# Two buffers for the recurrence's output gate, and stage waits for the PSUM banks that come next

## The reference

```
h = rmsnorm(x) ; x = x + 1/2 * rmsnorm(swiglu(h))            # FFN 1, 2816 hidden
h = rmsnorm(x) ; z = h @ W_in                                # one wide projection
  A: attention, 3 groups (window, dilation) x 8 heads of 64, merged by their softmax sums
  B: 8 heads, each 128 wide, both directions, in chunks of 64 tokens:
       S_t = diag(f_t) S_{t-1} + k_t v_t^T ;  o_t = S_t^T q_t
       o = rmsnorm(o_fwd + o_bwd) * silu(g_h)                # g_h: the output gate
  y = (sigmoid(gate_a) * (A @ P_A) + sigmoid(gate_h) * (B @ P_B)) @ W_out
x = x + rmsnorm(y)
h = rmsnorm(x) ; x = x + 1/2 * rmsnorm(swiglu(h))            # FFN 2
```

## Time and profile before

| | |
|---|---|
| median of 3 runs | 1547.39 us (1547.31 to 1548.15) |
| the profiled execution, its own time | 1546.26 us |
| its span in the profile | 1544.4 us |
| mean granted TensorE clock | 0.994 |
| TensorE matmul busy | 1497.4 us, 97% |
| TensorE weight load busy | 1227.5 us, 79% |
| VectorE busy | 719.4 us, 47% |
| ScalarE busy | 577.2 us, 37% |
| GpSimd busy | 23.5 us, 2% |
| chain that ended last, by engine | PE 94%, ACT 2%, DVE 2%, issue 1% |

### The profile page before, as it was taken

How to read it: one execution, slowest core, us unless ns; L and a number is a source line. 1 busy time by engine, 2 the same in 40 slices (tenths; PEclk the granted TensorE clock), 3 DMA queues, 4 the chain that set the end, 5 groups by cost and what they waited for, 6 DMA issues and landing times.

```text
span 1544.4 us, 20203 instructions
## 1 busy us (share of the span) xinstructions
PE 1497.4 (97%) x7610; PEld 1227.5 (79%) x7610; DVE 719.4 (47%) x1087; ACT 577.2 (37%) x840; POOL 23.5 (2%) x29
## 2 busy tenths in 40 slices
PE   7999999999999999999999999999999999999996
PEld 6888888887987777777887777778876888888885
DVE  6444444224644444443246665654446444443223
ACT  5223323223533444433244554553344332323221
POOL 0000000000100000000000000000000000000001
PEclk9999999999999999999999999999999999999998
DMA  5332222222422222212222221222231222222222
GB/s 182 99 98 95 95 95 95 96 95 82 145 88 90 86 69 86 69 59 92 95 82 69 68 76 60 68 69 96 83 106 57 95 95 95 95 95 95 96 96 82
DMA packets 39186, 138.65 MB, mean 90 GB/s; under 512 B 4535, under 2 KB 4535, under 8 KB 39095
## 3 DMA queue, kind: packets, MB, share of 16 engines
q1 hardware_dynamic: 37440, 132.14, 25.9%
q0 software_dynamic: 1552, 5.76, 1.3%
q10 hardware_dynamic: 144, 0.04, 0.0%
HBM read 135.75 MB, written 2.17 MB: 89 GB/s over the span
## 4 chain that ended last, share of the span: by engine, by line
PE 94%; ACT 2%; DVE 2%; issue 1%; DMA 0%; DVEq 0%; ACTq 0%
PE ps L258 27%; PE ps L259 26%; PE ps L260 26%; PE ps L605 2%; PE ps L848 2%; PE ps L861 2%; PE ps L607 1%; PE ps L606 1%; PE ps L831 1%; PE ps L766 1%; PE ps L768 1%; PE ps L767 1%; PE ps L1147 1%; ACT whi L248 1%; PE ps L1164 1%
## 5 line engine op out<-in xcount | busy, mean ns | idle before, releaser
L258 PE MATMUL ps<-hh,whi 128*128 128x512 f32 x1280 | 510.2, 399 | 26.7 <-DVE hl L520 12.7
L259 PE MATMUL ps<-hl,whi 128*128 128x512 f32 x1280 | 501.1, 391 | 0.0
L260 PE MATMUL ps<-hh,wlo 128*128 128x512 f32 x1280 | 500.8, 391 | 0.0
L248 ACT ACTIVATE whi<-raw 128x1024 fp32r<-128x1024 f32 x242 | 256.1, 1059 | 613.2 <-PE ps L260 552.3
L253 DVE TENSOR_TENSOR wlo<-raw,whi 128x1024 fp32r<-128x1024 f32 x242 | 296.3, 1225 | 396.2 <-ACT whi L248 396.2
L258 PEld LDWEIGHTS ps<-hh,whi 128*128 128x128 f32 x1280 | 241.6, 189 | 88.0 <-issue 28.2
L260 PEld LDWEIGHTS ps<-hh,wlo 128*128 128x128 f32 x1280 | 241.6, 189 | 51.6
L259 PEld LDWEIGHTS ps<-hl,whi 128*128 128x128 f32 x1280 | 241.8, 189 | 48.0 <-issue 0.2
L258 PE MATMUL ps<-ah,whi 128*128 128x512 f32 x352 | 137.1, 389 | 0.8 <-DVE tmp L365 0.8
L259 PE MATMUL ps<-al,whi 128*128 128x512 f32 x352 | 137.0, 389 | 0.0
L260 PE MATMUL ps<-ah,wlo 128*128 128x512 f32 x352 | 136.9, 389 | 0.0
(11 more groups left out here) (216 smaller groups left out, 1528.2 us busy)
## 6 DMA issues: line engine op xcount, KB each, us to landing
raw<-in_wstream SPq DMA_DIRECT2D x244, 512.0 KB, 3.3
bias<-vec_dram POOLq DMA_DIRECT2D x8, 576.0 KB, 6.6
xt<-in_x_t SPq DMA_DIRECT2D x8, 256.0 KB, 5.6
out_t<-xt SPq DMA_DIRECT2D x8, 256.0 KB, 2.0
cst<-in_consts POOLq DMA_DIRECT2D x1, 640.0 KB, 4.9
hot_sb<-in_onehot POOLq DMA_DIRECT2D x1, 297.0 KB, 4.1
vec_dram<-vec_sb POOLq DMA_DIRECT2D x1, 72.0 KB, 2.9
par<-in_params ACTq DMA_DIRECT2D x1, 40.5 KB, 4.1
```

Source lines behind the costliest of these rows:

```text
L248: nc.scalar.activation(whi[:, s, :], raw[:, s, :], ACT.Copy).then_inc(head_done, 1)
L258: nc.tensor.matmul(out, w, m, start=start, stop=False)
L259: nc.tensor.matmul(out, w, ml, start=False, stop=False)
L260: return nc.tensor.matmul(out, wl, m, start=False, stop=stop)
```

## The change

The output gate is made at the end of its own turn, behind the last `head` of that turn, into one of two buffers by the turn's parity (`gate`, and `tmp[:, 1, :]`, which exists already). The loops of ScalarE and VectorE over the turns 2 to 7 become three passes over two turns each; TensorE's loop stays. The v stage's copies out of PSUM are placed ahead of the conversion of the next weight block. Four waits of TensorE between stages become smaller, later or go.

```
+        gates = [gate[:], tmp[:, 1, :]]
...
             for b in range(4):          # v_act; v_dve alike with block_tail
-                if b > 1:
-                    block_head(1, b)
                 if b == 3:
                     leave(1, 0)
                     leave(1, 1)
+                if b > 1:
+                    block_head(1, b)
...
             turn(0, True, False, False)          # hgrn_pe
+            pe.wait_ge(sem("ih_out1"), 5)
             turn(1, True, True, False)
...
-            def turn(h, proj, scan, finish):          # hgrn_act
+            def turn(h, parity, proj, scan, finish):
...
                 if scan:
-                    if finish:
-                        act.wait_ge(sem("b_done"), h)
-                    nc.scalar.activation(gate[:], ps[:, 1, :], ACT.Silu).then_inc(sem("gate_done"), 1)
                     for d in range(2):
...
                 if proj:
                     head(act, first + 2 * h + 1, 1)
-                if not own:
+                if own:
+                    act.wait_ge(block_done, 2 * (first + 2 * h) + 4)
+                    nc.scalar.activation(gates[1 - parity], ps[:, 1, :], ACT.Silu).then_inc(sem("gate_done"), 1)
+                else:
                     nc.scalar.activation(first_gates[3], ps[:, 1, :], ACT.Sigmoid).then_inc(sem("sig_g"), 1)
...
-            with act.Fori(2, GH_HEADS) as h:
-                turn(h, True, True, True)
-            turn(GH_HEADS, True, True, True)
+            with act.Fori(1, GH_HEADS // 2) as two:          # hgrn_dve alike
+                turn(2 * two, 0, True, True, True)
+                turn(2 * two + 1, 1, True, True, True)
+            turn(GH_HEADS, 0, True, True, True)
...
-                nc.vector.scalar_tensor_tensor(out=b_out, in0=ps[:, 5, :], scalar=par[:, 48:49], in1=gate[:],
+                nc.vector.scalar_tensor_tensor(out=b_out, in0=ps[:, 5, :], scalar=par[:, 48:49], in1=gates[parity],
...
-            pe.wait_ge(sem("y_a"), 8)
+            pe.wait_ge(sem("y_a"), 6)
             ih_pe(pe, 2)
             pe.wait_ge(sem("ih_out0"), 5)
-            pe.wait_ge(sem("ih_out1"), 5)
             hgrn_pe(pe)
             gate_h_pe(pe)
-            pe.wait_ge(sem("y_h"), KT)
+            pe.wait_ge(sem("y_h"), KT - 1)
+            pe.wait_ge(sem("sig_h_done"), 4)
             columns_pe(pe, "w_out", "post2", KT, yh, yl, sem("yl_done"), 0)
...
             ffn_in_pe(pe, 3)
-            pe.wait_ge(sem("up"), 2 * FT)
             columns_pe(pe, "ffn3_out", "post3", FT, ah, al, sem("a_tail"), 1 + FT)
```

More of the change, by code:

```diff
@@ L725, in v_dve @@
             for b in range(4):
-                if b > 1:
-                    block_tail(1, b)
                 if b == 3:
@@ L730, in v_dve @@
                     leave(1, 3)
+                if b > 1:
+                    block_tail(1, b)
                 h_norm(2 * b)
@@ L1249, in turn @@
                     head(act, first + 2 * h + 1, 1)
-                if not own:
+                if own:
+                    act.wait_ge(block_done, 2 * (first + 2 * h) + 4)
+                    nc.scalar.activation(gates[1 - parity], ps[:, 1, :], ACT.Silu).then_inc(sem("gate_done"), 1)
+                else:
                     nc.scalar.activation(first_gates[3], ps[:, 1, :], ACT.Sigmoid).then_inc(sem("sig_g"), 1)
             nc.scalar.preload_act_table(ACT.Silu)
-            turn(0, True, False, False)
-            turn(1, True, True, False)
-            with act.Fori(2, GH_HEADS) as h:
-                turn(h, True, True, True)
-            turn(GH_HEADS, True, True, True)
-            gates = FIRST["gate_h"]
-            head(act, gates, 0)
+            turn(0, 0, True, False, False)
+            turn(1, 1, True, True, False)
+            with act.Fori(1, GH_HEADS // 2) as two:
+                turn(2 * two, 0, True, True, True)
+                turn(2 * two + 1, 1, True, True, True)
+            turn(GH_HEADS, 0, True, True, True)
+            head(act, FIRST["gate_h"], 0)
             b_head(GH_HEADS)
@@ L1291, in state_queries, with gated @@
                                         ALU.mult).then_inc(sem(f"q_st{d}"), 1)
-            def gated(h):
+            def gated(h, parity):
                 dve.wait_ge(sem("o_turned"), h)
                 dve.wait_ge(sem("gate_done"), h)
-                nc.vector.scalar_tensor_tensor(out=b_out, in0=ps[:, 5, :], scalar=par[:, 48:49], in1=gate[:],
+                nc.vector.scalar_tensor_tensor(out=b_out, in0=ps[:, 5, :], scalar=par[:, 48:49], in1=gates[parity],
                                                op0=ALU.mult, op1=ALU.mult).then_inc(sem("b_done"), 1)
@@ L1305, in b_tail, with turn @@
                                         ALU.subtract).then_inc(sem("bl_done"), 1)
-            def turn(h, proj, scan, finish):
+            def turn(h, parity, proj, scan, finish):
                 own = h is not GH_HEADS
@@ L1311, in turn @@
                 if finish:
-                    gated(h - 1)
+                    gated(h - 1, 1 - parity)
                 if scan:
@@ L1379, in turn @@
                         state_queries(h, d)
[L1381 to L1386, removed]
+            turn(0, 0, True, False, False)
+            turn(1, 1, True, True, False)
+            with dve.Fori(1, GH_HEADS // 2) as two:
+                turn(2 * two, 0, True, True, True)
+                turn(2 * two + 1, 1, True, True, True)
+            turn(GH_HEADS, 0, True, True, True)
+            gated(GH_HEADS, 0)
             tail(dve, FIRST["gate_h"], 0)
```

## The result

| | before | after |
|---|---|---|
| median | 1547.35 us, 4 runs (1546.57 to 1548.15) | 1527.51 us, 4 runs (1526.33 to 1527.76) |
| ratio | | 0.9864, 95% interval 0.9852 to 0.9877 |
| span of the profiled execution | 1544.4 us | 1525.6 us |
| mean granted TensorE clock in it | 0.994 | 0.995 |

The change takes 19.8 us, 1.4%, off the median. 1526.7 us had been predicted.

What follows compares the result with a forecast made beforehand. TensorE, busy for 97% of the span with one stream of matmuls, was taken to bound the kernel. The removed stalls and clock fall sum to 20.7 us, so 1547.39 us becomes 1526.7 us, range 1524.0 to 1531.5 us.

Steps and rivals of the forecast that it cites:

- v stage: Third group of the v stage: copying each PSUM bank once done removes TensorE's whole stall, 2.63 us.
- gate_a to ih: Boundary from gate_a to ih: waiting for 6 readings instead of 8 removes the stall, 1.45 us.
- ih to the recurrence: Before the recurrence's first block: the count of banks 2 and 3 is needed only in turn 1, saving 1.17 us.
- turn 1: Part 1 of the recurrence's turn 1: the gate's wait goes, but VectorE's `tail` is late next, saving 0.63 us.
- turns 2 to 7 and turn 8: Ahead of part 1: an earlier silu removes the gate stall, 8.4 us for six turns and 2.65 us in turn 8.
- clock behind turn 8: Part 1 of turn 8: with the stall gone, TensorE's clock no longer falls, saving 1.58 us.
- end of B's projection: Start of W_out: its first column needs banks 4 to 7, not bank 0, saving 1.15 us.
- FFN 2's up half: FFN 2's up half: its wait, which FFN 1 does not have, goes, saving 1.05 us.
- a longer first matmul: In the v stage's term: the first matmul after the stall takes 0.60 us instead of 0.40, adding 0.20 us.
- Rival 3: ScalarE's and VectorE's doubled loops need code fetches, six of 4.1 us, giving 1551.3 us; chance 0.02.
- Rival 2: In the turns, another wait (weights' low half) replaces the gate's, keeping half the stall: 1532.2 us; chance 0.08.
- Rival 1: The clock's fall does not follow from turn 8's stall, or falls elsewhere: gain 19.1 us, 1528.3 us; chance 0.14.

Runs made afterwards that it cites:

- buffer alone: Changed kernel with two gate buffers kept but the silu back at its old place in the next turn: 1531.62 us, ratio 0.9893.
- late gate: Changed kernel with only the last output gate (head 7) made in turn 8 behind `b_done` and its table loads, as before: 1532.92 us.
- v stage alone: Kernel before with only the v stage's copies out of PSUM moved ahead of the conversion: 1546.26 us, ratio 0.9983.
- the one with the waits changed: Kernel before with the changed waits between stages and the v stage's new order, the gate as before: 1538.99 us, ratio 0.9937.
- gate part alone: Changed kernel with the v stage's order and the waits between stages put back as before: 1534.65 us, ratio 0.9907.
- the last experiment: Kernel before with only turn 8's two activations exchanged, gate silu ahead of sigmoid: 1545.33 us, ratio 0.9985.
- the further stalls removed: Changed kernel plus attention's last block half, turn 0's block 3 conversion and the low part in two norms moved earlier: 1524.55 us, ratio to before 0.9847.

## Why the prediction was right

The mechanism was the one that was put first: one stream of matmuls, and each stall that the waits name taken out of it. Term by term, from the starts of the same matmuls in both profiles:

| term | predicted us | measured us |
|---|---|---|
| v stage | 2.63 | 2.37 (2.66 - 0.29) |
| gate_a to ih | 1.45 | 1.4 |
| ih to the recurrence | 1.17 | 1.2 |
| turn 1 | 0.63 | 0.6 |
| turns 2 to 7 and turn 8 | 8.4 + 2.65 | 11.2 (216.62 - 205.44) |
| clock behind turn 8 | 1.58 | 1.54 (7.24 - 5.70) |
| end of B's projection | 1.15 | 1.2 |
| FFN 2's up half | 1.05 | 1.1 |

Their sum is 20.6 us against 20.7. From the first matmul of the v stage, which both kernels reach by the same program, the span took 1166.2 us (1544.4 - 378.2) before and 1145.8 us (1525.6 - 379.8) after: 20.4 us. The profiled execution after reached that matmul 1.6 us later than the one before did, and then 0.28 us of that came back in the first matmuls, at the lower clock in both. All the profiles of this study reach it between 378.1 and 380.0 us, whatever the kernel, so that is how one execution differs from the next, and the 0.8 us by which the forecast was missed lies within it. There is some luck in the base that it started from, three runs with a median of 1547.39 us: the other groups of the same kernel have medians from 1547.69 to 1548.53.

**The v stage's term was too large by 0.26 us.** The step "a longer first matmul" took 0.60 us against 0.40 for a mark of the stall. The first matmul of the third group shows 0.60 us without a stall too, so it belongs to the place. At the other stage boundaries that excess did go, 0.50 to 0.39 us at W_out.

**The costs put at nothing were nothing.** The silu at the end of the turn fits into ScalarE's idle time; the doubled loops cost no time, alone (ratio 1.000) or against straight code (0.2 us). Rival 3 had six fetches of up to 4.1 us: none shows. The Trainium skill ("Runtime: NRT & Kernel Launch", Instruction fetch mechanics) names a fetch only for a taken branch whose target is not in the window, and the doubled loop's even stalls agree with that; by the prediction's count of the loop's body no run here leaves that window, so none tests it.

**Rival 2 fell** where it was put, in the turns 2 to 7, and held in turn 1 alone, as the sum had it. The study with one engine's copies moved shows what it would have looked like: 2.0 us of stall behind the other engine.

**Rival 1 was half right.** "With the stall gone I expect the fall to go" held: no profile of a kernel without the long stall in turn 8 shows a fall there. But the stall does not always cost a fall, as the one row had it: of the six profiles with a stall of 2.63 us it was there in five (before, doubled loops, buffer alone, late gate, v stage alone), where part 1 of turn 8 takes 7.0 to 7.3 us, and absent in the one with the waits changed, with 5.67. And the v stage's stall, which the prediction took for harmless on the strength of one profile, was followed by a fall in one profile of four. The groups of the kernel before scatter over 5 us and those of the changed kernel over 2, and the upper part of that scatter went when the v stage's stall did. Against the 0.994 runs of the kernel before (1546.1 to 1548.6 us) the change gives about 19.6 us, against the others some 22. The Trainium skill ("TensorE: Matmul & The Clock Gate", Part 1) has the gate's timing run free of the kernel's start; 2.27 us of idle time at the same place with the clock at 1.00 behind it in three profiles and at 0.70 in a fourth agree with that.

**The halves do add up.** The 23.1 us come from medians of before with the upper group in them. In three profiles without a fall behind the v stage's stall and with the shorter time at the lower clock at FFN 2's start, the time from the first matmul of the v stage is 1166.6 us with the doubled loops alone (1546.0 - 379.3), which is the kernel before in all but those, 1153.3 with the gate part alone (1532.9 - 379.6) and 1145.8 with the whole change (above). That is 13.3 us for the gate part and 7.5 for the rest, 20.8 in all, where the terms said 13.3 and 7.4. Why the four runs with the gate part alone had no upper group is not shown: they keep the v stage's stall, and with that stall the last experiment's runs fell into two groups, so it may be chance.

**What stays open:** whether the upper group of the kernel before has one fall more or two. Its mean clock is 0.002 to 0.003 lower, but none of its members was profiled. The last experiment's profile, of the longest of its runs, has two things that the profile of the kernel before, of its lower group, has not: the fall in the v stage, which costs 1.4 us there (262.52 us from the third group to the wait in attention, for 261.11 before), and a longer time at the lower clock from FFN 2's start, 1.1 us (250.81 for 249.69). So v's fall alone need not be what parts the two groups. And the v stage's copies moved alone brought the lower end down by 1.5 us instead of 2.4; its profile spans 1544.4 us with the whole gain of the v stage in it (49.57 us for 51.74 up to the third group), and 1.4 us more in the stretch from FFN 2's start on, where the longer time at the lower clock is seen again.

## What to carry to other kernels

Where one engine is busy nearly all the time, list the waits ahead of its instructions and ask of each which buffer or bank the next instruction really needs; a stall costs somewhat more than its idle time: in this kernel 0.1 us more in the v stage, about 0.3 us at the four other stage boundaries (by the table above), and under 0.1 us a turn behind the small matmuls. Where the consumer of a buffer is also what delays its next producer, a second buffer can be worth the whole stall, as in the turns 2 to 7 here, where the old place in the program was in time by 0.3 us; in turn 1 and turn 8, where the producer's engine is late for another reason, it took the new place too. Look behind the releaser that the view gives: of the v stage's 2.27 us, 2.01 would have stayed with the other engine.

## What the hardware showed beyond what was expected

The clock of TensorE after a stall is not a property of the stall's length alone. In the recurrence, behind 1.4 us of idle time, it never fell in these profiles (32 stalls); behind 2.27 us in the v stage it stayed at 1.00 in three profiles and was 0.70 on average over the next 5.66 us in a fourth; behind 2.63 us it fell in five profiles of six; behind 5.08 us, or 4.63 with the further stalls removed, it always fell, and the time at 1.2 GHz differed (0.80 and 0.65 on average over 8 us for one and the same kernel).

The place counts too. At the start of the v stage TensorE idles for only 1.38 us, or 0.93 with the further stalls removed, and there the clock falls in all 14 profiles, between 0.6 us before the start of the first matmul and 0.8 us behind it. Ahead of that idle time stand 3.6 us of small matmuls, in the kernel before:

```profile
373.17 3.62 PE L284 MATMUL ps<-hot_sb,table 33*8 33x256 f32 x18
378.17 0.79 PE L605 MATMUL ps<-whi,hh 128*128 128x512 f32 x1 [1.38 <-issue]
```

The first 24 matmuls of 512 columns behind it take 7.0 to 7.4 us in 13 of the profiles and 8.5 in the other (only ScalarE's copies moved), where part 1 of turn 2 takes 5.66. No experiment changed these small matmuls, so whether the small matmuls are the reason is not shown.

So executions with the same stalls to 0.01 us differ by 1 to 3 us, and a single profile neither shows nor excludes such a fall.
